# Constant products on TensorE ahead of some of its waits, in a three-block float32 model on one core

## The reference, cut to what matters

```python
x = first_block(x, ...)    # attention + state-space mixer, two layers
x = second_block(x, ...)   # conv + attention mixer, then a mixture of 64 experts
return third_block(x, ...) # two attentions (MLA and forgetting), gated and merged
```

```python
g = jnp.argmax(grp_logits, axis=-1)          # one of 8 groups
top_v, top_i = lax.top_k(sel, TOP_K)         # two of its 8 experts
expert_ids = g[:, None] * EXPERTS_PER_GROUP + top_i
...                                          # rows sorted into blocks of one expert
return (jax.nn.silu(xb @ w1[e]) * (xb @ w3[e])) @ w2[e]
```

## Time and profile before

| | us |
|---|---|
| median of 3 runs | 2108.41 |
| lowest, highest run | 2108.34, 2121.31 |
| the profiled execution's own time | 2118.97 |
| its span from first to last instruction | 2117.2 |
| TensorE products busy | 1714.6 (81% of the span) |
| VectorE, ScalarE busy | 592.9 (28%), 264.1 (12%) |
| bytes moved | 553.35 MB |

### The profile page before, as it was taken

The page is one execution under the profiler, slowest core; times in us unless marked ns, Lnnn a source line. Parts: engine busy times, 40 slices in busy tenths (PEclk is TensorE's granted clock), DMA queues, the critical chain, the costliest instruction groups (busy, mean ns, idle before and its releaser), DMA issues.

```text
span 2117.2 us, 21233 instructions
## 1 busy us (share of the span) xinstructions
PE 1714.6 (81%) x9244; PEld 1048.5 (50%) x9244; DVE 592.9 (28%) x1394; ACT 264.1 (12%) x695; POOL 11.5 (1%) x35
## 2 busy tenths in 40 slices
PE   8989899899899999866676576666667666999888
PEld 6665566655468887432233232222233231468655
DVE  0365432654423321410111111110111110116542
ACT  0232212321102100100100000000000001122210
POOL 0000000000000000000000000000000000000000
PEclk9999999999999999997888888788888888999979
DMA  9422253329334365499999999999999999444000
GB/s 351 137 80 81 80 180 128 111 94 303 120 128 156 123 239 199 164 428 429 427 427 427 427 428 427 427 428 427 427 428 428 426 429 384 179 170 170 18 0 20
DMA packets 106614, 553.35 MB, mean 261 GB/s; under 512 B 7856, under 2 KB 10416, under 8 KB 82960
## 3 DMA queue, kind: packets, MB, share of 16 engines
q1 hardware_dynamic: 105664, 548.81, 65.4%
q0 software_dynamic: 848, 3.05, 0.4%
HBM read 550.79 MB, written 1.05 MB: 261 GB/s over the span
## 4 chain that ended last, share of the span: by engine, by line
PE 63%; DMA 27%; DVE 6%; ACT 3%; issue 1%; SPq 0%; DVEq 0%; ACTq 0%
PE bank L629 33%; DMA ring<-in_w 16%; DMA arena<-in_w 11%; PE bank L1087 7%; PE bank L638 5%; PE bank L1108 4%; PE bank L1060 3%; PE bank L617 2%; PE bank L849 1%; DVE arena L1935 1%; ACT arena L1451 1%; PE bank L675 1%; PE bank L841 1%; PE bank L780 1%; PE bank L760 0%
## 5 line engine op out<-in xcount | busy, mean ns | idle before, releaser
L629 PE MATMUL bank<-arena,ring 128*128 128x256 f32 x1856 | 417.8, 383 | 2.7 <-DVE arena L2760 2.2
L1087 PE MATMUL bank<-ring,arena 128*32 128x512 f32 x1216 | 279.2, 723 | 156.4 <-DMA ring<-in_w 103.9
L629 PE MATMUL bank<-ring,arena 128*128 128x512 f32 (+5 forms) x1000 | 380.5, 535 | 15.2 <-ACT arena L1383 3.0
L629 PEld LDWEIGHTS bank<-arena,ring 128*128 128x128 f32 x1856 | 353.5, 192 | 55.9 <-issue 7.4
L1087 PE MATMUL bank<-arena 128*32 128x512 f32 x832 | 226.4, 713 | 97.2 <-DMA ring<-in_w 50.0
L629 PEld LDWEIGHTS bank<-ring,arena 128*128 128x128 f32 x1000 | 186.7, 198 | 182.3 <-issue 151.6
L1087 PEld LDWEIGHTS bank<-ring,arena 128*32 128x32 f32 x1216 | 71.3, 130 | 278.9 <-issue 278.9
L1060 PE MATMUL bank<-arena 128*128 128x128 f32 x512 | 126.4, 419 | 29.7 <-DVE arena L2472 28.6
L1087 PEld LDWEIGHTS bank<-arena 128*32 128x32 f32 x832 | 57.3, 129 | 177.1 <-issue 176.8
L1060 PEld LDWEIGHTS bank<-arena 128*128 128x128 f32 x512 | 123.3, 335 | 43.4 <-DVE arena L2472 41.3
L1108 PE MATMUL bank<-ring,arena 128*32 128x512 f32 x608 | 111.1, 599 | 7.3 <-ACT arena L1654 5.4
(11 more groups left out here) (368 smaller groups left out, 1250.9 us busy)
## 6 DMA issues: line engine op xcount, KB each, us to landing
ring<-in_w SPq DMA_DIRECT2D x114, 2048.0 KB, 31.0
arena<-in_w SPq DMA_DIRECT2D x78, 2048.0 KB, 30.9
ring<-in_w_in SPq DMA_DIRECT2D x42, 2048.0 KB, 8.0
ring<-in_w_out SPq DMA_DIRECT2D x6, 2048.0 KB, 8.0
ring<-in_w_ada SPq DMA_DIRECT2D x6, 2048.0 KB, 7.9
ring<-in_w_out SPq DMA_DIRECT2D x16, 512.0 KB, 9.0
ring<-in_w_conv_out SPq DMA_DIRECT2D x2, 2048.0 KB, 7.8
ring<-in_w_attn_out SPq DMA_DIRECT2D x2, 2048.0 KB, 7.9
```

The costliest lines, as they stand in the source:

```text
L629: i = te.matmul(ps, lhsT, rhs, start=n0 + k == 0, stop=n0 + k == n - 1)
L1087: m = te.matmul(ps[32 * j:32 * j + 32, :], LM.xg[:, f, 128 * k + 32 * j:128 * k + 32 * j + 32], vs[j][:, 512 * (k % 2):512 * (k % 2) + 512 ...
```

## The change

A helper `warm(ps, n)` issues n products of constants, `ones` with the 256 columns of `distm`, into a bank whose contents are overwritten by the products that follow. `held(ps, n, *names)` does that and then waits for the names. They are placed

- in `mixer_rank`: nine ahead of the wait for `("chosen", 1)`, two between the rank product and the count; the opening of bank 2 moves ahead of the nine;
- in `by_parts`: five ahead of each of the waits for quarters 2 and 3 of the last group's w2 (into bank 4);
- in `last_block`: for each token tile, three ahead of the wait for `("un3", tt)`, with the opening of the first turned bank ahead of them; and three ahead of the wait for both evictions of the turned tokens, with the opening of qb's bank ahead of them. The waits themselves move into `turn` and `tok`; qb's weight is now waited for ahead of them.

```diff
+            def warm(ps, n):
+                t.wait_ge(*at.of("dist"))
+                for _ in range(n):
+                    te.matmul(ps[:, 0:256], ones[:, :], distm[:, :], start=True, stop=True)
+
+            def held(ps, n, *names):
+                warm(ps, n)
+                ready(*names)
+
-            def turn(group, pairs, b=None):
+            def turn(group, pairs, b=None, hold=None):
                 ps = fresh(*group, b=b)
+                if hold:
+                    held(ps, *hold)
                 t.wait_ge(*at.of("const"))
...
-            def turn_T(name, src, tt, strided=False):
+            def turn_T(name, src, tt, hold=None):
...
+                         b=2 * tt + j, hold=None if j else hold)
...
-            def tok(group, srcT, wv, tt, n, o=0, kc=8):
-                i = product(fresh(*group)[:, 0:n], tok_pairs(srcT, wv, tt, o, n, kc))
+            def tok(group, srcT, wv, tt, n, o=0, kc=8, hold=None):
+                ps = fresh(*group)
+                if hold:
+                    held(ps, *hold)
+                i = product(ps[:, 0:n], tok_pairs(srcT, wv, tt, o, n, kc))
                 i.then_inc(*t.done("mm", *group))
...
             def mixer_rank():
+                ps = fresh("count", b=2)
+                warm(ps, 9)
                 t.wait_ge(*at.of("chosen", 1))
                 te.matmul(P[3][:, 0:64], tris[:, :], LM.mk[:, 1, :], start=False, stop=True
                           ).then_inc(*t.done("mm", "rank", 1))
-                ps = fresh("count", b=2)
+                warm(ps, 2)
...
                         for q in range(4):
+                            if w == 2 and q > 1:
+                                warm(P[4], 5)
                             name, v = unit(4 * w + q)
...
                 for tt in range(2):
-                    ready(("un3", tt))
-                    turn_T(("hT3",), L3.un, tt)
-                    ready(*both("hT3", tt))
+                    turn_T(("hT3",), L3.un, tt, hold=(3, ("un3", tt)))
                     for name, n in firsts:
                         t.wait_ge(*at.of("w", (name,)))
-                        tok((name, tt), hT, weights((name,), n), tt, n)
+                        tok((name, tt), hT, weights((name,), n), tt, n,
+                            hold=(3, *both("hT3", tt)) if name == "qb" else None)
```

More of the change, by code:

```diff
@@ L618, in turn @@
                 i.then_inc(*t.done("mm", *group))
-            def turn_T(name, src, tt, strided=False):
+            def turn_T(name, src, tt, hold=None):
                 for j in range(2):
-                    turn((*name, tt, j), [
-                        (128 * i, src[:, tt, 4 * j + i:1024:8] if strided else
-                         src[:, tt, 128 * (4 * j + i):128 * (4 * j + i) + 128]) for i in range(4)], b=2 * tt + j)
+                    turn((*name, tt, j), [(128 * i, src[:, tt, 128 * (4 * j + i):128 * (4 * j + i) + 128]) for i in range(4)],
+                         b=2 * tt + j, hold=None if j else hold)
             def product(ps, pairs, n0=0, n=None):
```

## The result

The changed kernel is slower: 2120.75 us median of 16 runs (2117.33 to 2127.53) against 2114.0 us for the kernel before (16 runs, 2108.34 to 2121.31). The ratio is 1.0037, 95% interval 1.0023 to 1.005, which is +7.8 us (+4.9 to +10.6); the two medians lie 6.75 us apart. The median of three that the forecast started from, 2108.41, was low; the lowest run of the changed kernel lies 9 us above the lowest of the kernel before. The forecast was 2107.8 us, in a range up to 2117.0, with -0.6 us for the change: too low in level by 5.6 us and in the difference by some 8 us. That the change stays within 1% was right.

A forecast was written before the change was run, and what follows sets the result against it. It took the expert weight stream to bound the middle up to 1790.41 us, then TensorE's products. Terms -0.26 - 1.3 + 0 + 1.3 + 1.3 + 1.3 - 2.95 = -0.6 us took 2108.41 to 2107.8, range 2103.0 to 2117.0.

The forecast's parts named there:

- The choice of experts: In mixer_rank: nine products fit the wait, the rank product runs at full clock, and -0.26 us passes through the weight stream.
- The last weight: Last w2: quarter 3 takes 1.92 us instead of 3.31 at full clock, starting 0.1 us late: -1.3 us.
- The products in block 3: Three products free ahead of tile 0's turn; +1.3 us ahead of tile 1's turn and of each tile's qb.
- What the clock gives back: Block 3, tile 1: the clock holds, so its 48 records take 15.69 us instead of 18.64: -2.95 us.
- The later stretch: Rival, chance 0.13: clock falls shift at 2005.14 to 2037.05 us, worth up to 13 us; near 2120 us.
- The rule named there: Skill's free-running monitor, cited for the rival that clock falls differ between runs: no fall 0.22, both tiles 0.12.

The follow-up runs named there:

- block3_free: Kernel before with only block 3's constant products, written into free bank 4 ahead of the waits, none ahead of tile 1's turn: 2112.7 us, ratio 0.9997.
- the nine profiles above: Four profiles of the kernel before, four with 2, 4, 8 or 9 constant products inserted at the gate, and late_hold; tile 1's records 17.1 to 18.7 us.
- before_3: Third profile of the kernel before, nothing changed: scatter to gate 44.09 us, gate to end 271.32 us.
- before_4: Fourth profile of the kernel before, nothing changed: scatter to gate 44.24 us, gate to end 271.48 us.
- late_hold: Kernel before with constant products only in the softmax waits of block 3's late attention: 2105.64 us, ratio 0.9945.
- best: Kernel before with choice and last weight as changed, block 3's first products as in block3_free, late attention held: 2102.35 us, ratio 0.9928.

## Why the prediction was wrong

*The choice of experts* (-0.26): right up to the gather, 2.36 us behind the rank product instead of 2.62. That it is passed on through the stream is not shown; the run with it alone can't show so little.

*The last weight* (-1.3): wrong in the change as a whole. The clock was won as forecast, from quarter 3's start to the scatter 1797.50 - 1794.10 = 3.40 us against 4.76. But the forecast had quarter 3 start 0.1 us late, and it started 1.21 to 1.33 us behind its landing in the three profiles of the changed kernel: from quarters 0 and 1 to quarter 3 the chain on TensorE took 1794.10 - 1783.97 = 10.13 us where the forecast had 9.67, since five products take 2.35 us and not 2.2, and the transfer landed 8.80 to 8.92 us behind the start of quarters 0 and 1, not 9.53. From landing to scatter the changed kernel takes 4.61 to 4.73 us, the kernel before 4.53 to 4.80: nothing was gained.

*The products in block 3* (1.3 three times): right, and for the forecast reason. Ahead of tile 0's turn they were free (0.35 us idle left), ahead of tile 1's turn they pushed it (0.26 us idle as before, then 1.4 us more), and ahead of qb `fresh` put them behind the wait. block3_free shows the other side.

*What the clock gives back* (-2.95): this is the step that failed most, in two ways. Its size was of one profile: three later ones show 17.06 to 17.21 us for tile 1's records, so that the fall costs 1.4 to 1.5 us or 2.95, about equally often in the nine profiles above. And the assumption that the clock holds was made for tile 1 by comparison with tile 0, whose own clock was taken for granted: there it now falls, at +1.5 to +1.6 us. Against the cheaper size the two cancel: scatter to gate went from 44.2 to 48.30 us, +4.1, the 3.9 us of products and nothing returned. Against the first profile's 45.67 it is +2.6 where the forecast had 3.9 - 2.95 = +0.95. Why the clock falls in tile 0 is answered as far as above: its products begin some 10 us after the scatter's start instead of 8.45, behind idle time that nothing fills.

*The later stretch*: named as a rival with 0.13 and a price of 13 us, as a matter of luck. The runs showed it to be a part of the change's cost: gate to end 273.4 against 271.3 to 271.5, +1.9 us, against three of the four profiles of before, and 3 us less than the first profile's 276.36. A delay was taken to pass on at its own price; here 0.87 us of delay cost 5.3 (2.1 to 8.5).

From the rank product to the end the changed kernel takes 1240.9 to 1241.0 us in its three profiles, and the kernel before 1235.0 to 1235.1 in three of its four: +5.9 us, inside the measured +4.9 to +10.6. It is made up of -0.1 up to the scatter, +4.1 to the gate and +1.9 behind it. Against the first profile, with its 1241.9, it is -1.0 us. So the forecast of -0.6 lies close to what happened to the very execution it was made from, but by luck, since its parts were -0.6, +2.6 and -3.0 us where it had -1.6, +0.95 and 0. How often each form of the kernel before occurs over many executions was not seen, so how the +7.8 us of the runs divide into these parts stays open.

*The level.* Three runs were too few: the 16 runs of before have 2114.0 as their median, 5.6 us above the three. With that level the forecast would have been 2113.4, and still 7 us short. What spreads the executions most lies ahead of all three places: the rank product starts at 875.33, 877.34, 878.11 and 882.96 us in the four profiles of before, of one and the same program, and the 4.9 us between the spans of before_3 and before_4 (2113.1 and 2118.0) is this start.

The rule named there, from the Trainium skill ("TensorE: Matmul & The Clock Gate", Part 1), that the monitor is free-running and slow products vary from run to run, agrees with the four profiles of before: 18.64 and three times about 17.2 us for the same records, and one fall or two later. The same page's advice to keep TensorE busy ("Why this matters for your kernels") agrees with late_hold and best, where filled waits kept the clock at 1.00.

## What to carry to other kernels

Look first for the wait that ends the idle time you mean to fill. If the products that should fill it open the bank that is being evicted, they stand behind the wait and only cost: here 3.9 us paid, against nothing paid when they went to a free bank. Nor should more products be put ahead of a wait than fit into it: five ahead of a wait of 0.80 us made the last weight late by as much as the clock gave back. Fill first the waits whose clock loss is largest on TensorE's own chain: a stretch of many small products at 0.51 over 32 us was worth about 10 us (gate to end 261.2 against 271.3 to 271.5), the three places of the change, with the products of block 3 well placed, another 3 (best against late_hold). And where short waits alternate with work, compare several profiles before a loss of clock is priced from one.

## What the runs showed of the hardware

The clock fell after the constant products and not before them: at 1.00 through 1.9 us of idle time and 1.4 us of products, and at 0.50 in the window from 1807.40 to 1809.40. The same pattern with the products ahead of the idle time kept 1.00 (15.69 and 15.66 us for 48 records). Two traces in which tile 0's products began equally late, 10.03 and 10.08 us after the scatter's start, differ there only in the constant products: with 1.64 and 1.82 us idle around the turn the clock fell (17.37 us for the 48 records), with these waits filled down to 0.35 and 0.52 us it didn't (15.69 us).

And a delay can cost more than itself: two constant products of 0.87 us in a place without any wait made the kernel 5.3 us slower (2.1 to 8.5).
